# Unread TensorE products in four waits, and an earlier first gathered half tile, in a one-core hybrid layer

## The reference, cut to what matters

```python
x = _layer_norm(ALPHA * x + g1 * y, ln1_g, ln1_b)
f = _moe(x * (1 + sc2) + sh2, w_router, b_router, w_gate, w_up, w_down)
x = _layer_norm(ALPHA * x + g2 * f, ln2_g, ln2_b)

hg = jnp.einsum('btd,edf->btef', h, w_gate)
hu = jnp.einsum('btd,edf->btef', h, w_up)
act = jax.nn.silu(hg) * hu * combine[..., None]
return jnp.einsum('btef,efd->btd', act, w_down)
```

## Time and profile before

| what | us |
|---|---|
| median of three runs | 736.07 |
| the three runs | 740.06, 735.64, 736.07 |
| the profiled execution, whole time | 738.71 |
| its span, first to last instruction | 737.0 |
| TensorE, share of the span busy | 93% |
| TensorE, mean granted clock | 0.975 |

### The profile page before, as it was taken

One profiled execution on the slowest core, in us unless ns is written; L12 is line 12 of the kernel. 1 busy time (PEld: TensorE's weight loads), 2 busy tenths in 40 slices (PEclk: granted clock), 3 DMA queues, 4 the chain that ended last, 5 costly groups with the idle time before them and its releaser, 6 DMA issues.

```text
span 737.0 us, 12612 instructions
## 1 busy us (share of the span) xinstructions
PE 684.4 (93%) x4858; PEld 551.4 (75%) x4858; DVE 574.8 (78%) x840; ACT 430.9 (58%) x602; POOL 57.0 (8%) x88
## 2 busy tenths in 40 slices
PE   4699999999899999999998999999999999999881
PEld 2488988898689889944457878888888888888640
DVE  2749998798992467665388998999999999989765
ACT  1646967173133536550034589888888888888721
POOL 2060000000011000131001400000000000000310
PEclk9899999999999999999998999999999999999996
DMA  9999496455758698899716899999999999999332
GB/s 320 352 254 356 152 390 233 166 195 202 273 180 286 235 396 316 311 329 256 236 42 252 325 377 400 399 399 398 398 398 399 398 399 398 399 398 360 102 130 85
DMA packets 91324, 219.17 MB, mean 297 GB/s; under 512 B 3339, under 2 KB 3635, under 8 KB 91271
## 3 DMA queue, kind: packets, MB, share of 16 engines
q1 hardware_dynamic: 84928, 199.24, 74.0%
q0 software_dynamic: 5840, 18.94, 7.6%
q10 hardware_dynamic: 503, 0.28, 0.1%
HBM read 179.08 MB, written 39.36 MB: 296 GB/s over the span
## 4 chain that ended last, share of the span: by engine, by line
PE 75%; DVE 15%; ACT 3%; DMA 3%; issue 2%; SPq 1%; DVEq 0%; ACTq 0%
PE ps L1187 72%; DMA ring<-in_w_in 3%; PE ps L1608 2%; DVE w_lo L1771 2%; DVE arena L1931 1%; DVE arena L1930 1%; DVE arena L1876 1%; PE ps L1627 1%; ACT w_hi L836 1%; SPq L553 1%; DVE arena L2331 1%; DVE arena L2099 1%; DVE arena L2333 1%; DVE ln_stats L2090 0%; DVE arena L2089 0%
## 5 line engine op out<-in xcount | busy, mean ns | idle before, releaser
L2237 DVE TENSOR_TENSOR w_lo<-arena,w_hi 128x1024 fp32r<-128x1024 f32 x96 | 114.6, 1220 | 8.6 <-ACT w_hi L1071 7.4
L2237 DVE TENSOR_TENSOR w_lo<-ring,w_hi 128x1024 fp32r<-128x1024 f32 x92 | 109.9, 1220 | 9.8 <-ACT w_hi L1071 9.1
L1187 PE MATMUL ps<-h_hi,w_lo 128*128 128x384 f32 x288 | 101.8, 353 | 8.9 <-DVE w_lo L1771 7.0
L1071 ACT ACTIVATE w_hi<-arena 128x1024 fp32r<-128x1024 f32 x96 | 101.1, 1064 | 14.9 <-PE ps L1187 14.7
L1071 ACT ACTIVATE w_hi<-ring 128x1024 fp32r<-128x1024 f32 x92 | 96.6, 1063 | 19.2 <-PE ps L1187 19.0
L1187 PE MATMUL ps<-w_hi,slot_tokens_lo 128*128 128x512 f32 x256 | 102.6, 401 | 0.8 <-DVE w_lo L2237 0.8
L1187 PE MATMUL ps<-w_hi,slot_tokens_hi 128*128 128x512 f32 x256 | 100.2, 391 | 0.0
L1187 PE MATMUL ps<-w_lo,slot_tokens_hi 128*128 128x512 f32 x256 | 99.8, 390 | 0.0
L1187 PE MATMUL ps<-h_lo,w_hi 128*128 128x384 f32 x288 | 97.3, 338 | 0.0
L1187 PE MATMUL ps<-h_hi,w_hi 128*128 128x384 f32 x288 | 97.3, 338 | 0.0
L1771 DVE TENSOR_TENSOR w_lo<-ring,w_hi 128x1024 fp32r<-128x1024 f32 x44 | 53.9, 1230 | 24.1 <-ACT w_hi L836 23.0
(11 more groups left out here) (378 smaller groups left out, 1112.5 us busy)
## 6 DMA issues: line engine op xcount, KB each, us to landing
slot_rows<-arena SPq DMA_DIRECT2D x12, 2048.0 KB, 18.2
ring<-in_w_in SPq DMA_DIRECT2D x11, 2048.0 KB, 10.4
ring<-in_w_ada SPq DMA_DIRECT2D x10, 2048.0 KB, 9.3
ring<-in_w_up SPq DMA_DIRECT2D x8, 2048.0 KB, 14.1
arena<-in_w_up SPq DMA_DIRECT2D x8, 2048.0 KB, 14.4
ring<-in_w_down SPq DMA_DIRECT2D x8, 2048.0 KB, 10.4
arena<-in_w_gate SPq DMA_DIRECT2D x8, 2048.0 KB, 14.7
arena<-in_w_down SPq DMA_DIRECT2D x8, 2048.0 KB, 11.2
```

What stands on the lines that cost most here:

```text
L1071: act.activation(w_hi[:, at_ % 4, :], raw[:, q * QUARTER:(q + 1) * QUARTER], ACT.Copy).then_inc(S["hi_ready"], 1)
L1187: return pe.matmul(out, lhsT, rhs, start=start, stop=stop, skip_group_check=open_)
L2237: tt(w_lo[:, at_ % 4, :], raw[:, q * QUARTER:(q + 1) * QUARTER], w_hi[:, at_ % 4, :].bitcast(F32), ALU.subtract).then_inc(S["lo_dve"], 1)
```

## The change

`keep_running` is moved up so that all parts of PE's list can call it, and takes a bank. Twenty-one products are added in three waits ahead of the first `part` job, in bank 6; seven ahead of the last half tile's turn in the norm; in routing the three groups go from 6, 6 and 4 products to 8, 11 and 7; in the last expert three are put ahead of the turn of its activation and five behind it, in bank 7. None of these 46 products is read. In the mixing, the two gathered products of tile 1's first half are put first, ahead of tile 0.

```diff
+            def keep_running(products, bank=2):
+
+                for _ in range(products):
+                    mm(ps[:, bank, 0:P], ident, ident)
...
                     if (q, k0) == (0, 0):
                         pe.wait_ge(S["consts_made"], 2)
+                        keep_running(9, 6)
+                        pe.wait_ge(S["h_hi"], 2)
+                        keep_running(8, 6)
+                        pe.wait_ge(S["hi_ready"], 1)
+                        keep_running(4, 6)
                     w = weights(q)
...
                 for half in range(2):
+                    if half and i == NT - 1:
+                        keep_running(7)
                     pe.wait_ge(S["x_ready"], 2 * i + half + 1)
...
-            keep_running(6)
+            keep_running(8)
             pe.wait_ge(S["sexp_ready"], NT)
-            keep_running(6)
+            keep_running(11)
             pe.wait_ge(S["mask_ready"], 1)
...
             last.then_inc(S["ranks_ready"], 1)
-            keep_running(4)
+            keep_running(7)
...
                 for q in range(4):
                     gate_up(n, 4 + q, q, 1, 4)
+                pe.wait_ge(S["last_sel_sb"], 1)
+                keep_running(3, 7)
                 act_transpose(n)
+                keep_running(5, 7)
...
-            for i in range(NT):
-                for half, bank in enumerate(MIX_BANKS[i]):
-                    if i == 0:
-                        pe.wait_ge(S["out_sb"], 2 * NE - 1 + half)
-                    cols = slice(half * G, (half + 1) * G)
-                    if i:
-                        pe.wait_ge(picked[i], 32)
-                        for c in range(2):
-                            mm(ps[:, bank, :], pick_diag[:, c, i - 1, :], PICK[:, c, i, cols], c == 0, False)
-                    mm(ps[:, bank, :], last_T[:, i, :], OUT[1][:, cols], i == 0, True).then_inc(S["mixed"], 1)
+            def picks_mixed(i, half):
+
+                cols = slice(half * G, (half + 1) * G)
+                pe.wait_ge(picked[i], 32)
+                for c in range(2):
+                    mm(ps[:, MIX_BANKS[i][half], :], pick_diag[:, c, i - 1, :], PICK[:, c, i, cols], c == 0, False)
+
+            def last_mixed(i, half):
+
+                cols = slice(half * G, (half + 1) * G)
+                mm(ps[:, MIX_BANKS[i][half], :], last_T[:, i, :], OUT[1][:, cols], i == 0, True).then_inc(S["mixed"], 1)
+
+            picks_mixed(1, 0)
+            for half in range(2):
+                pe.wait_ge(S["out_sb"], 2 * NE - 1 + half)
+                last_mixed(0, half)
+            last_mixed(1, 0)
+            picks_mixed(1, 1)
+            last_mixed(1, 1)
+            for half in range(2):
+                picks_mixed(2, half)
+                last_mixed(2, half)
```

More of the change, by code:

```diff
@@ L1565, in _ @@
             turned_rows(NT - 1)
-            def keep_running(products):
-                for _ in range(products):
-                    mm(ps[:, 2, 0:P], ident, ident)
-            keep_running(6)
+            keep_running(8)
             pe.wait_ge(S["sexp_ready"], NT)
-            keep_running(6)
+            keep_running(11)
             pe.wait_ge(S["mask_ready"], 1)
```

## The result

The kernel after takes 739.30 us (median of 22 runs, 737.29 to 744.13), the kernel before 736.38 us in its 22 runs (733.33 to 740.18). The ratio is 1.0042, 95% interval 1.0026 to 1.0059: slower by 2.9 us, where 734.4 was forecast. The profiled execution after took 743.58 us, with a span of 741.8.

What follows compares the result with a forecast made beforehand. TensorE's own work was taken to bound the kernel (three quarters of the chain, VectorE 15%), slowed by 1.2 GHz stretches. -0.5 + 0.1 - 1.2 + 0 + 0 = -1.6 us, from 736.07 to 734.4, range 731.8 to 736.9.

Steps and rivals of the forecast that it cites:

- Ahead of the projection: 21 products before the projection hide in TensorE's waits and hold the clock up: -0.5 us, bounds 0 and 1.5.
- What follows up to 45.76 is TensorE's list in order, so 0.5 us goes on.: Behind the projection's start, TensorE works in order up to 45.76 us, so the 0.5 us gained is carried on.
- the start at 27.75 stays: The added products end at 27.2 us, before the first real product of the projection, whose start at 27.75 us is unchanged.
- Norm, +0.1: Seven products take 1.56 us against a 1.36 us wait before the last half tile's turn, overrunning by 0 to 0.2.
- Routing, -1.2: Nineteen products before the mask hold the clock; ranks come sooner and VectorE waits less: -1.2 us, bounds 0.3 and 1.2.
- With the gap filled to 0.7 us I expect 2.4 GHz to hold: In routing, nineteen products leave TensorE 0.7 us idle before the mask instead of 1.97, so its clock stays at 2.4 GHz.
- The products overrun their wait: Rival: routing's nineteen products run partly at 1.2 GHz and end 2.7 us late, total 738.4 us; chance 0.08.
- The gathering: In routing, 96 gathering instructions take 10.7 us (sign of being right: 10.7 to 11) instead of 12.2.
- the 0.94: VectorE's idle 0.94 us at 420.63 us, behind a ScalarE rounding that waits for TensorE, was to disappear.
- Experts, last expert, mixing, all 0: Routing's gain passes through the experts; the last expert's products fit its idle time; the conditional hides the mixing's new order.
- the first rival: Slow stretches fall elsewhere: the last down product runs partly at 1.2 GHz, 1.7 us lost without the products; 732.7 us, chance 0.17.
- -1.6: Sum over the kernel in us: -0.5 projection, +0.1 norm, -1.2 routing, 0 last expert, 0 mixing.

## Why the prediction was wrong, and where it was right

**The step that failed** stands under "Ahead of the projection": "What follows up to 45.76 is TensorE's list in order, so 0.5 us goes on." The products were priced by their time alone, and everything behind them was taken to run as before. But 84 instructions in front move all that follows through the blocks in which instructions are loaded, and some 100 us further on the fastest run of the program met the end of a block at a worse place: +3.0 us (3.66 - 0.62). That it is the places, and not the products, the kernel with 84 empty instructions shows (3.78 us of gaps). No rival had it, and "issue" in the waits of the kernel before was read only at the mixing. The Trainium skill, "Runtime: NRT & Kernel Launch", Instruction fetch mechanics, has instructions streamed in blocks of 256 and calls the cost "mostly hidden". The 256 agree with the places of the gaps; hidden it was not in this run of small products, with stops of up to 2.41 us.

**Ahead of the projection, -0.5.** The real products ran at 1.00, but not because the clock stayed up. In this execution everything ahead was slow, and the first record of the clock is a 1.00 that begins at 26.1, while the added products ran. Before, the first of these lines took 1.93 us and the second 1.50:

```profile
16.92 3.64 PE L1187 MATMUL ps<-ring,silu_w 128*32 128x256 f32 x32
...
22.22 2.80 PE L1313 MATMUL ps<-small,arena 128*128 128x128 f32 x12
24.82 5.48 PE L1187 MATMUL ps<-small 128*128 128x128 f32 x42
30.05 0.42 PE L1187 MATMUL ps<-h_hi,w_lo 128*128 128x384 f32 x1
```

The products ended at 30.3, a microsecond after the remainder they were to wait for, so "the start at 27.75 stays" failed too, and the 28.80-us stretch began at 46.96. With only the first 21 the clock did stay up, from 14.4 to 137.3 us. Over the traces the stretch began at 46.2 to 47.2 with the products (seven) and at 45.8 to 47.5 without (seven), so nothing arrived there. Yet the way itself is shorter: from the start of the first remainder (`w_lo`) to the stretch it is 18.7 to 19.2 us with the products and 19.3 to 20.2 without. It is the first remainder that came later, at 27.4 to 28.3 against 26.4 to 27.3; how much of that the products cause is open.

**Norm, +0.1.** In four of five traces the seven products fitted, with 1.50 us of waiting left behind them: 0. The forecast's 1.36 us is the wait of an execution whose clock fell in the norm; where it had not fallen, the wait without the products is 3.07. In the one trace with the products whose clock fell there (the kernel without the first 21) no wait was left.

**Routing, -1.2.** Wrong as a whole at "With the gap filled to 0.7 us I expect 2.4 GHz to hold". It held in one trace of five, the only one whose clock had fallen in the norm, as in the trace that the forecast was made from; there B is 1.2 us shorter, as forecast. In the other four, where it fell ahead of the nineteen, what happened is the rival named last but one ("The products overrun their wait"), to which I gave 0.08: the ranks 0.9 to 1.5 us late, where it said up to 2.7. The gathering did take 10.98 us (forecast 10.7 to 11) and the 0.94 was gone, but both are also found without the products, in the five traces whose clock fell ahead of the twelve and was back for the gathering. Over all traces B is 1.0 us longer with the products (median of five 371.0, of nine 370.0), of which the measured times show no more than a few tenths, within their noise.

**Experts, last expert, mixing, all 0.** Right: C is 39.98 before and after. The conditional was near 4.8 us (4.62) and the first mixing product stood behind it, as written; turning it round showed that it, and not the evictions, held the mixing. What the first rival says of the last expert was seen in three of the six traces without its products: the last down product took 7.2 to 7.3 us instead of 5.8, 1.4 to 1.5 lost where the rival said 1.7.

**The sum.** For the parts together I said -1.6. With the instructions put back in place they measured -2.7 to +0.3 us, so their sum is not refuted, though the routing term in it won or lost with the course of the clock; as far as the sum fits, that is partly luck. The result is this plus the stops, 3.0 us, which I had at nothing.

## What to carry to other kernels

An instruction that hides in a wait still takes a place. Before adding some, look in the timeline for "issue" in the middle of equal, very short instructions, count a weight load with each MATMUL, and see which products the edit pushes onto the next 256th place; satisfied waits at the head of a list are a cheap way to try it. Not every "issue" is the end of a block: one of 0.54 us at about 200 us stands ahead of the same product in all fourteen traces, wherever the blocks end. And one trace of a kernel shows one course of the clock: the forecast for routing was made from one that five of nine traces do not share. And where a rare branch lies between two busy stages, put the common path directly behind the comparison.

## What the runs showed of the hardware that I had not expected

- TensorE's list stops at places 256 instructions apart (32 + 64 + 160 between the first two gaps of the kernel after) when the instructions behind the stop are not there yet: up to 2.41 us each. It goes on 1.2 to 1.5 us behind a 16 KB transfer of the instruction queue. The profile page's 34 transfers of this queue, q8, are 0.56 MB, of the same number before and after. What sets off the loading of the next block, and how long ahead, was not tried.
- 84 idle instructions at the start of the kernel before cost 2.7 us by ratio (0.0037); 172 instructions (43 small products) at the start of the kernel after gave back 3 to 4.
- The comparison took 78 ns where its common path stood behind it and 4812 where it had to jump. In all eight traces with the jump it ended 1.3 to 1.5 us behind a 16 KB transfer of q8. The rule of the Trainium skill, "Runtime: NRT & Kernel Launch", Instruction fetch mechanics, that a taken branch whose target is not held waits until it is fetched, agrees with both.
- At the start the granted clock of a window isn't to be trusted: the transposes at 22.2 us of the kernel after took 2.80 us, those of the kernel before 1.50, and both windows say 1.00. The records of the clock begin at 14.2 us before and at 26.1 after; ahead of them the view shows 1.00, whatever the products' times say.
- In one trace the clock fell right behind such a stop: 0.50 for 3.4 us behind the 2.41 us of the kernel with only the first 21. Behind the stops of 2.01 and 2.13 us it did not. That the stop is the cause is not shown.
